# Hyena filter spectra moved from the Hyena blocks into the first modulation product

## The reference, cut to what matters

```python
mod = silu(cond) @ w_ada + b_ada            # (2 conditions) x (2048 -> 6*2048); sh1, sc1, gt1, sh2, sc2, gt2
h = rmsnorm(x, g_pre_mix) * (1 + sc1) + sh1
proj = h @ w_in                             # q, k, v, g of the GLA heads, then u_hy (3 x 1024 Hyena channels)
# filters: of the weights alone, neither of x nor of h
hdn  = sin(freq * (pe @ w1 + b1)); hdn = sin(freq * (hdn @ w2 + b2))
filt = (hdn @ w3).reshape(L, 2, 2, 1024) * exp(-t01 * deltas)   # two directions, two orders, 1024 channels
filt = filt / sum(abs(filt), axis=(0, 1))
filt_f = rfft(concat(filt[:, 0], 0, flip(filt[1:, 1])))         # the filter's spectrum
# the Hyena channels
z = parts[0]
for n in range(2):
    conv = irfft(rfft(z, n=2*L) * filt_f[n], n=2*L)[:L]
    z = parts[n + 1] * (conv + hy_bias[n] * z)
```

## Time and profile before

| | |
|---|---|
| median of 3 runs | 1558.45 us (1552.96 to 1559.66) |
| span of the profiled execution (first to last instruction) | 1555.7 us |
| busy: PE, DVE, ACT, POOL | 1409.3, 748.9, 241.6, 74.0 us |
| mean transfer rate over the span | 271 GB/s |
| chain that ended last: PE, DMA, DVE | 70%, 17%, 8% of the span |
| `w_ada` loads of the ring | 16 of 2048 KB, 11.9 us from issue to landing |

### The profile page before, as it was taken

One profiled execution on the slowest core, in us unless ns is written; L12 is line 12 of the kernel. 1 busy time (PEld: TensorE's weight loads), 2 busy tenths in 40 slices (PEclk: granted clock), 3 DMA queues, 4 the chain that ended last, 5 costly groups with the idle time before them and its releaser, 6 DMA issues.

```text
span 1555.7 us, 14305 instructions
## 1 busy us (share of the span) xinstructions
PE 1409.3 (91%) x5328; PEld 652.8 (42%) x5328; DVE 748.9 (48%) x1269; ACT 241.6 (16%) x401; POOL 74.0 (5%) x126
## 2 busy tenths in 40 slices
PE   2679999999999899999999999799899978999886
PEld 0135544444555455555544444533333333333332
DVE  0148888997775887968883723600000000000005
ACT  2101320100011111111211012511111110111014
POOL 3010000000010000000000000000000000000001
PEclk9889999999999999999999999899999988899899
DMA  9998457876669543221327734899999999999996
GB/s 347 428 371 264 144 181 258 275 241 220 201 200 321 173 143 97 80 88 63 134 69 293 232 112 163 310 395 404 411 375 388 405 400 396 398 389 381 405 425 276
DMA packets 132945, 422.20 MB, mean 271 GB/s; under 512 B 9897, under 2 KB 75668, under 8 KB 115032
## 3 DMA queue, kind: packets, MB, share of 16 engines
q1 hardware_dynamic: 120292, 375.79, 64.8%
q0 software_dynamic: 6496, 33.38, 6.3%
q10 hardware_dynamic: 6096, 12.20, 2.1%
HBM read 407.96 MB, written 22.58 MB: 277 GB/s over the span
## 4 chain that ended last, share of the span: by engine, by line
PE 70%; DMA 17%; DVE 8%; issue 3%; ACT 2%; ACTq 0%; POOL 0%; DVEq 0%; POOLq 0%; SPq 0%
PE ps L501 19%; PE ps L504 19%; PE ps L890 11%; DMA s_mem<-in_w_exp_gate 11%; PE ps L910 6%; DMA s_mem<-in_w_ada 3%; PE ps L775 3%; DVE s_mem L1767 2%; PE ps L672 1%; PE ps L448 1%; DMA s_mem<-in_hy_freq 1%; PE ps L623 1%; PE ps L430 1%; DMA y_slots<-s_mem 1%; DVE s_mem L1739 1%
## 5 line engine op out<-in xcount | busy, mean ns | idle before, releaser
L1593 DVE SCALAR_TENSOR_TENSOR s_mem<-s_mem,s_sT 128x512 f32<-128x512 f32 x480 | 339.4, 748 | 34.1 <-DMA s_mem<-in_w_ada 17.7
L501 PE MATMUL ps<-s_mem 128*128 128x384 f32 x1024 | 343.9, 493 | 1.1 <-DVE s_mem L1624 1.1
L504 PE MATMUL ps<-s_mem 128*128 128x512 f32 x672 | 292.8, 594 | 0.7 <-ACT s_mem L1364 0.7
L890 PE MATMUL ps<-s_mem 128*64 128x512 f32 x1152 | 263.5, 614 | 28.8 <-DMA s_mem<-in_w_exp_gate 27.6
L501 PEld LDWEIGHTS ps<-s_mem 128*128 128x128 f32 x1024 | 194.0, 192 | 143.4 <-issue 17.7
L504 PEld LDWEIGHTS ps<-s_mem 128*128 128x128 f32 x672 | 126.3, 190 | 158.5 <-issue 157.6
L890 PEld LDWEIGHTS ps<-s_mem 128*64 128x64 f32 x1152 | 91.1, 141 | 198.4 <-issue 198.4
L2059 DVE TENSOR_TENSOR s_mem<-s_mem,ps 64x512 f32<-64x512 f32 x18 | 12.2, 679 | 312.3 <-ACT s_mem L1462 312.3
L910 PE MATMUL ps<-s_mem 128*64 128x512 f32 x576 | 153.1, 693 | 9.3 <-DVE s_mem L2061 9.3
L910 PEld LDWEIGHTS ps<-s_mem 128*64 128x64 f32 x576 | 45.6, 157 | 103.5 <-issue 91.6
L2066 DVE COPY s_mem<-ps 128x512 f32<-128x512 f32 x18 | 12.4, 691 | 149.4 <-PE ps L910 149.4
(11 more groups left out here) (290 smaller groups left out, 1007.6 us busy)
## 6 DMA issues: line engine op xcount, KB each, us to landing
s_mem<-in_w_ada SPq DMA_DIRECT2D x256, 256.0 KB, 3.4
s_mem<-in_w_exp_gate SPq DMA_DIRECT2D x32, 2048.0 KB, 26.3
s_mem<-in_w_exp_up SPq DMA_DIRECT2D x32, 2048.0 KB, 31.2
s_mem<-in_w_exp_down SPq DMA_DIRECT2D x32, 2048.0 KB, 30.6
s_mem<-in_w_in SPq DMA_DIRECT2D x24, 2048.0 KB, 8.9
s_mem<-in_w_ada SPq DMA_DIRECT2D x16, 2048.0 KB, 11.9
s_mem<-in_w_out SPq DMA_DIRECT2D x8, 2048.0 KB, 8.2
y_slots<-s_mem ACTq DMA_DIRECT2D x34, 256.0 KB, 11.3
```

Source lines behind the costliest of these rows:

```text
L501: m = mm(ps[:, banks[m_], 0:TOK], v[:, k, m_ * P:(m_ + 1) * P], hT[:, kk, :], start=(kk == 0), stop=(kk == KT - 1))
L504: m = mm(ps[:, banks[m_], :], hT[:, kk, m_ * P:(m_ + 1) * P], v[:, k, :], start=(kk == 0), stop=(kk == KT - 1))
L890: m = mm(ps[half, 0, :], hgT[:, kh * 8 + k, :], weights(e, 2 * kh + which)[:, k, :], start=(kh + k == 0), stop=(kh * 8 + k == KT - 1), ski ...
L1593: v.op(ve.scalar_tensor_tensor(out=o, in0=w, scalar=scale, in1=o, op0=ALU.mult, op1=ALU.add), S("piece_used") if last else None)
```

## The change

The filter code leaves the Hyena blocks. All four spectra are computed during the first modulation product, in the places between its 16 steps, with another layout of the work, and stored to DRAM (`spec_dram`, 1.5 MB each). In a Hyena block only one transfer of 1.5 MB remains, which POOL issues once the spectrum before has been read (`G_read`).

- ACT's queue loads all of `w3`, all of the decay (`k_decay`) and the four forward tables first; the tokens `x` come after these.
- Taps: 6 matmuls a filter as before, into banks 2 to 5. Norms: 12 matmuls of 128 columns that use 32 array columns each, one reciprocal of 256 elements a row on DVE (before: two of 512), and 8 matmuls (`filter_scales`) that spread the result over the partitions, copied by ACT.
- The sums and differences of the two directions (6 of 128 x 512) and of the even and odd parts (4) are done on POOL (`taps_combined`, `spectrum_combined`), not on DVE.
- Spectrum 0 is stored in the modulation stage, since it lies in `hT`; ACT waits for it before the first copy of turned tokens. Spectra 1 to 3 are stored after the small loads that wait for `h_modulated`; ACT waits for them before it copies `q`, and DVE before the decays.
- `x` is scaled in place. `wdec` is zeroed after the filters.

The core of the diff:

```diff
@@ PE, first modulation product
             for k in range(KT):
                 ada_step()
-                if k == KT - 8:
-                    pe.wait_ge(S("hid_ready"), 1)
-                    take(pe, 3, "hid2")
-                    mm(ps[:, 3, 0:TOK], w2s, ftmp[0:HID, 1, :], start=True, stop=True).then_inc(filled("hid2"), 1)
+                if k < 2:
+                    hidden_layer(k + 1)
+                elif k == 2:
+                    filter_taps(0)
+                elif k == 3:
+                    pe.wait_ge(S("in_rowsB"), 32)
...
+                elif k == 4:
+                    filter_norms(0)
+                elif k == 5:
+                    filter_taps(1)
+                elif k == 6:
+                    filter_scales(0)
+                    filter_spectrum(0)
+                elif k == 7:
+                    filter_norms(1)
+                elif k == 8:
+                    filter_taps(2)
+                elif k == 9:
+                    filter_scales(1)
+                    filter_spectrum(1)
                     pe.wait_ge(S("x_scaled"), NT)
...
+                elif k == 14:
+                    x_turns(range(15, KT))
+                    filter_scales(3)
+                    filter_spectrum(3)
@@ PE, new helpers
+            def filter_norms(ho):
...
+                pe.wait_ge(S("absf_ready"), NT * (ho + 1))
+                take(pe, 4, f"norm{ho}")
+                for s, tiles in enumerate(TILES):
+                    for t in tiles:
+                        for j in range(4):
+                            m = mm(ps[32 * j:32 * j + 32, 4, s * P:(s + 1) * P], ones[:, 0:32],
+                                   fs[ho][:, t, j * P:(j + 1) * P], start=(t == tiles[0]), stop=(t == tiles[-1]),
+                                   skip_group_check=True)
+            def filter_scales(ho):
+                pe.wait_ge(S("norm_inverted"), ho + 1)
...
+                    for j in range(4):
+                        m = mm(ps[:, bank, j * P:(j + 1) * P], pick[:, j, :], norm_part[:, s, :], start=True, stop=True,
+                               skip_group_check=True)
@@ PE, Hyena block
                 if ho > 0:
                     conv_back(ho - 1)
-                filter_taps(ho)
-                project_half(*where, 1, readers=("act", "dve"), between=lambda: filter_norms(ho))
-                filter_spectrum(ho)
+                project_half(*where, 1, both)
                 for _ in hy_turn(hb, part):
                     pass
                 conv_ahead(ho)
@@ POOL
+            def taps_combined(ho):
+                pool.wait_ge(filled(f"norm{ho}"), uses[f"norm{ho}"][2])
+                g.op(nc.gpsimd.memset(ff[ho][0:1, 0:2, 1, :], 0.0))
+                g.sync()
+                for t in range(NT):
+                    plus, minus = ff[ho][:, t, 0, :], ff[ho][:, t, 1, :]
+                    g.op(nc.gpsimd.tensor_tensor(fs[ho][:, t, :], plus, minus, ALU.add), S("fsd_ready"))
+                    g.op(nc.gpsimd.tensor_tensor(plus, plus, minus, ALU.subtract), S("fsd_ready"))
+            def spectrum_combined(ho):
+                pool.wait_ge(S("spec_parts"), ho + 1)
...
+                    g.op(nc.gpsimd.tensor_tensor(minus, even, odd, ALU.subtract), S("spec_whole"))
+                    g.op(nc.gpsimd.tensor_tensor(even, even, odd, ALU.add), S("spec_whole"))
...
             pool.wait_ge(S("h_modulated"), 1)
             pool.dma_start(wlr, w_in[:, COL_LR:COL_LR + 2 * RANK].rearrange("(k p) n -> p k n", p=P)
...
+            for ho in range(1, N_FILT):
+                store_spectrum(ho)
...
+            for ho in range(N_FILT):
+                pool.wait_ge(S(f"spec_out{ho}"), 16)
+                if ho > 0:
+                    pool.wait_ge(S("G_read"), ho)
+                pool.dma_start(spectrum.rearrange("p r n -> p (r n)"), spec_dram[ho]).then_inc(S("in_spectrum"), 16)
@@ ACT
+            def x_columns(kts):
+                for kt in kts:
+                    b = read(act, f"xT{kt}")
+                    if kt == 0:
+                        act.wait_ge(S("spec_out0"), 16)
...
+            for ho in range(1, N_FILT):
+                act.wait_ge(S(f"spec_out{ho}"), 16)
             for m_ in range(4):
                 copy_out(f"q_{m_}", qf[:, m_, :])
@@ DVE
+            tap_products(0)
...
+            invert_norms(0)
+            tap_products(1)
+            spectrum_parts(0)
             inverse_roots(0, NT)
...
+            invert_norms(1)
+            tap_products(2)
+            spectrum_parts(1)
+            invert_norms(2)
+            tap_products(3)
+            spectrum_parts(2)
+            invert_norms(3)
+            spectrum_parts(3)
             mod_row(0)
             mod_row(1)
@@ DVE, Hyena block
-                filter_sums(ho, lambda: run(4))
+                run(4)
                 for m_ in range(4):
                     short_conv(hb, part, m_)
-                filter_spectrum(ho)
```

More of the change, by code:

```diff
@@ L623, in transform, with conv_ahead @@
                 mm(ps[:, bank, :], dft[:, table, :], src, start=True, stop=True).then_inc(filled(key), 1)
[L625 to L646 removed]
+            def conv_ahead(ho):
                 if ho == 0:
                     pe.wait_ge(S("in_dft"), 16)
[L650 to L656 removed]
                 if ho % 2:
@@ L1604, in run, with tap_products @@
                     next(ada)
+            sine_argument("hid2", 1, P)
+            def tap_products(ho):
+                hb = ho // 2
+                if ho == 0:
+                    dve.wait_ge(S("in_decay"), 16)
+                for t in range(NT):
+                    for d in range(2):
+                        key = f"f{ho}{t}{d}"
+                        b = read(dve, key)
+                        v.op(ve.tensor_tensor(ff[ho][:, t, d, :], ps[:, b, :], decay[:, t, hb * HALF:(hb + 1) * HALF],
+                                              ALU.mult), freed("dve", key))
+                for t in range(NT):
+                    dve.wait_ge(S("abs_done"), 2 * (NT * ho + t + 1))
+                    v.op(ve.tensor_tensor(fs[ho][:, t, :], fs[ho][:, t, :], other_abs[:, t, :], ALU.add), S("absf_ready"))
@@ L1627, in _ @@
             run(26)
+            for ho in range(1, N_FILT):
+                dve.wait_ge(S(f"spec_out{ho}"), 16)
             for d in range(2):
```

305 lines of the change are left out of this document (171 added, 134 removed).

## The result

The changed kernel is slower: 1568.51 us (median of 4 runs, 1566.28 to 1570.42) against 1559.06 for the kernel before (4 runs), a ratio of 1.0068 with a 95% interval of 1.0047 to 1.009. The forecast was 1536, with 1520 to 1558 as the range. The profiled execution has a span of 1565.4 us (before 1555.7).

The account below looks back on a forecast made before the run. It took the first modulation product as bound by transfers and the Hyena blocks by PE; -46.5 (blocks) + 23 (first stage) + 2 (projection) - 1 (clock) = -22.5 us, from 1558.45 to 1536, range 1520 to 1558.

Parts of the forecast that it names:

- The blocks: Hyena blocks: removing filter work from PE's path gains 28 + 17 + 1.5 = 46.5 us, bounds 43 to 49.
- The handover: Hyena blocks, between projection and turns: PE waits 2.6 us for the last channel's copy and short convolution.
- The first stage: First modulation product: the added filter work costs 23 us, bounds 11 and 35; the stage ends at 122.5.
- ACT's four more issues stand in front of `x`: First stage, ACT's queue: x lands later but PE first needs it at the tenth step, so no cost.
- the count of bytes at 413 GB/s: First stage: 5.5 MB more take 13 us, less about 2; used as the lower bound of its cost.
- The sum of 88: First stage: PE's work after 24.4 us totals 88 us, ending at 112.5 without waits.
- 10 us of waits in all: First stage: PE's waits for sine arguments, serial filter pieces and slots total 10 us, against 21.8 of slot waits before.
- The clock in front of the projection: First projection: a busy PE ahead should let it begin at 2.4 GHz, -1 us.
- POOL: right: First stage: POOL's combinations take 1.2 us each and stay just hidden up to about 1.4 us.
- The stores and the decays: Projection after the first stage: spectrum stores may delay DVE's w_ada pieces, costing 2 us, bounds -1.5 and 11.
- "Slower": Rival, 11%: first stage costs more than blocks gain; slow POOL combinations hold PE, 1584 us at 2.8 us each.
- the forecast's own signs: First stage, among others: w_ada waits under 10 us and DMA share below 0.95, showing PE took over as bound.

Follow-up runs that it names:

- e9: Changed kernel with w3, decay and x loaded on SP's queue and two spare matmuls before the turns of each block; 1550.31 us, ratio 0.9942.
- e4: Changed kernel with w3 and decay issued on SP's queue behind the first w_ada slot and x behind the third; 1555.42 us, ratio 0.997.
- e3: Changed kernel with ACT's squares of x moved behind the second filter's tap sizes and the first filter's scales; 1560.6 us, ratio 1.0008.
- e11: Changed kernel with w3 loaded by one transfer into 128 partitions instead of two into 64 (other filters); 1563.91 us, ratio 1.002.
- e8: Changed kernel with two spare 512-column matmuls into a free bank before the turns of each of the four blocks; 1563.73 us, ratio 1.0034.
- e12: e9 with w3 loaded by one transfer into 128 partitions (other filters); 1545.11 us, ratio 0.991 to the kernel before.
- e2: Changed kernel with POOL's 40 combinations cut from 512 to 8 elements a row (wrong filters); 1569.49 us, ratio 1.0065.

## Why the prediction was wrong

**The blocks: right, with one size missing.** 42.1 us (by p) against 46.5. The handover was to be 2.6 us; each of the four pauses is 2.4. The missing piece is the clock: after the pause PE has a granted clock of 0.81 in the stretch of a block's turns and transform, and 1.00 with two spare matmuls in it, which give back 5.2 us over the blocks. These are the lines of after (669.6 to 678.5) and of e9 (652.9 to 660.2):

```profile
669.60:678.50 8.90, 8.57 (x25) 4.63 (x26) 3.19 (x7) 2.28 (x4) 0.00 (x0) 0.81 0.55 210
```

```profile
652.90:660.20 7.30, 7.00 (x25) 3.84 (x26) 3.14 (x6) 2.28 (x4) 0.00 (x0) 1.00 0.67 253
```

Before, the six transforms to a spectrum stood between the projection and the turns, and PE paused there for 0.4 us.

**The first stage: wrong, and this decides.** The step that failed is "ACT's four more issues stand in front of `x`, which lands later; `x` is first needed on PE at the tenth step, so nothing", and with it the count of bytes at 413 GB/s whatever their form. The last step was to end at 122.5 and ended at 149.6. Of the difference, 7.9 us are PE's own work at a lower clock (95.9 against 88), and 19.4 us are idle PE (29.4 against 10). The sum of 88 itself was right: with fewer stops, in e9, PE is busy 87.7 us in the stage. Behind it 6.9 us passed to q instead of 3.8, some 2 of them the blur of the mark. The experiments price the causes:
- Where `w3`, decay and `x` queue: 15.8 us at p (e4). Two things lie in it. ACT squares `x` ahead of tap sizes that DVE and the norms wait for, up to 9.4 us of it (e3). I had looked at who needs `x` on PE and not at what stands behind `x` on ACT, in order. The rest is PE and DVE waiting for `w3` and the decay.
- The form of `w3`'s transfers: at p 0.7 to 3.2 us (e11, against e8 and after), 1.9 with the loads on SP (e12), hardly to be told from the spread of such a mark; what is shown is the rate, 243 against 421 GB/s. I divided bytes by the rate of 2 MB loads over 128 partitions.
- DVE beside POOL: 3 us at the scaling of `x` and 2 to 3 in front of q (e2), of which little reached the end of the stage.
- The bytes themselves, as I read it (no run prices them alone): 14 to 16 us of waits for `w_ada` remain in e4, e9 and e12. I had taken 10 us of waits in all. I had the sum of bytes (13 us) and treated it as a bound that PE's work would hide; but of the 5.5 MB the decay, `w3` and the tables (2.9) are wanted within the first third of the stage, where PE has little else.

These overlap, and their sum isn't the difference. In e12 the last product step ends at 133.0, still 10.5 us later than the 122.5 of the forecast, and the waits for `w_ada` there are 14.2 us. That these last waits come of the bytes is not shown.

**The clock in front of the projection: not as forecast.** The term of -1 us took it that a busy PE would enter the projection at 2.4 GHz. It pauses for the modulation rows and DVE in front of it: from 149.0 to 156.5 it is busy 1.95 us, and from 156.5 to 163.0 the granted clock is 0.53, as low as before (0.63 from 103 to 110).

**POOL: right.** A combination mostly takes 1.25 to 1.28 us (forecast 1.2, threshold 1.4), also beside DVE's products, which read PSUM. No matmul was released by POOL at a spectrum, only four weight loads, 0.9 us in all. Beside DVE's sums it takes 1.72 us and beside the scaling of `x` 2.25:

```profile
57.74 1.27 POOL L1168 TENSOR_TENSOR s_mem<-s_mem 128x512 f32<-128x512 f32 x1
...
88.32 2.25 POOL L1177 TENSOR_TENSOR s_mem<-s_mem 128x512 f32<-128x512 f32 x1
```

The slowdown of both was in the bounds, yet only as POOL's price; DVE's own was left out. The first combination took 1.27 us right behind a memset and shows nothing of the 6 us that the prediction named for a first call. The Trainium skill (GPSIMD Engine Reference, section "1. Specifications") says that the two engines share their SBUF interfaces, with contention for DVE instructions with two inputs in SBUF or in a two-port mode. The trace agrees: DVE's sums with both inputs in SBUF went from 684 to 1066 ns, its products with one input in PSUM stayed (682 and 683), and its `tensor_scalar` on SBUF went from 1283 to 2293 ns, though the trace doesn't name that one's mode.

**The stores and the decays: right.** The projection ran at 359 GB/s with a DMA share of 1.03, and PE's waits at the decays didn't grow (in e2 alone they did).

**The rivals.** "Slower" came true, but not by its mechanism: it was not POOL's pace. The rival missing from the list was a transfer that lands late behind a queue and holds an engine in the middle of its order. Two of the forecast's own signs came true all the same: PE's waits for `w_ada` fell to 3.5 us and the DMA share in the stage to 0.79. They didn't tell a PE that is busy from a PE that stands behind other engines.

## What to carry to other kernels

When loads are put ahead of another on a queue, work out the new landing time of each and list everything that stands behind its first waiter on every engine in order, not just who reads the data. A stage bound by transfers is the worst place for work that brings its own bytes; their time is their size over the rate of their own form, and here two loads into 64 partitions were not what one into 128 was. When work leaves a dense stretch of matmuls, look at the pause it opens: a spare matmul in it can be worth more than it costs. And before a difference at a mark is given to an edit, compare the mark in two profiles that have the same program up to it.

## What the runs showed of the hardware

- While two transfers of 512 KB into 64 partitions each (source rows 8 KB with gaps) were under way, all traffic was at 243 GB/s with the DMA engines busy; with one transfer into 128 partitions (rows without gaps) in their place it was at 421.
- Loads of 0.5 to 1.5 MB on one queue beside 2 MB loads on another landed late: the decay 39.4 us after its issue on ACT's queue, 15.8 on SP's behind one slot.
- A pause of 2.4 us on PE after dense work was followed by a lower granted clock in three of four blocks (transforms of 6.29, 6.59 and 7.49 us, and 5.41 in the last); one of 0.66 us in none.
- DVE and POOL on SBUF slow each other by up to 1.8 times, in both directions (2293 against 1283 ns, 2.25 against 1.27 us); DVE's products out of PSUM and POOL did not (683 against 682 ns, 1.25 us).
